# First block's feed-forward input as 24 units of seven half-size products, with two of the low halves made by GpSimd

## The reference, cut to what matters

```python
h = rmsnorm(x, norm_ffn[l])
x = x + conv_ffn(h, ffn_w_in[l], ffn_conv_w[l], ffn_conv_b[l], ffn_w_out[l])
```

## Time and profile before

| | |
|---|---|
| times of three runs | 2921.67, 2915.93 and 2917.06 us, median 2917.06 us |
| span of the profiled execution | 2915.5 us |
| its own time | given only among the three runs, not beside the span; the span is 1.6 us under their median |
| granted TensorE clock | 1.000 over the span (2.4 GHz level) |
| PE, PEld busy | 99%, 86% |
| DVE, ACT, POOL busy | 73%, 44%, 12% |

### The profile page before, as it was taken

How to read it: one execution, slowest core, us unless ns; L and a number is a source line. 1 busy time by engine, 2 the same in 40 slices (tenths; PEclk the granted TensorE clock), 3 DMA queues, 4 the chain that set the end, 5 groups by cost and what they waited for, 6 DMA issues and landing times.

```text
span 2915.5 us, 46310 instructions
## 1 busy us (share of the span) xinstructions
PE 2895.9 (99%) x16662; PEld 2505.6 (86%) x16662; DVE 2123.2 (73%) x3346; ACT 1275.7 (44%) x2027; POOL 356.7 (12%) x272
## 2 busy tenths in 40 slices
PE   9999999999999999999999999999999999999999
PEld 7888788778888888998887899988998887699987
DVE  8797674667766648888566887858888767688862
ACT  4653732342222225555233555625555236465541
POOL 0043340000000001110033011101110021011100
PEclk9999999999999999999999999999999999999999
DMA  4322123223323336773334477436774332257723
GB/s 142 98 94 94 58 95 122 73 80 125 98 94 96 99 94 170 184 185 101 108 109 130 122 182 184 118 109 173 187 184 110 103 109 80 80 156 179 187 78 108
DMA packets 129884, 356.97 MB, mean 122 GB/s; under 512 B 14608, under 2 KB 14864, under 8 KB 129360
## 3 DMA queue, kind: packets, MB, share of 16 engines
q1 hardware_dynamic: 103248, 303.14, 32.1%
q0 software_dynamic: 26496, 51.92, 10.4%
HBM read 352.90 MB, written 2.10 MB: 122 GB/s over the span
## 4 chain that ended last, share of the span: by engine, by line
PE 56%; DVE 3%; issue 1%; ACT 1%; DMA 1%; POOL 0%; DVEq 0%; SPq 0%; POOLq 0%; ACTq 0%
PE ps L1443 9%; PE ps L1445 9%; PE ps L1444 9%; PE ps L993 9%; PE ps L995 8%; PE ps L994 8%; PE ps L1667 0%; PE ps L1704 0%; PE ps L1158 0%; DMA cpad<-in_pairs 0%; PE ps L1147 0%; PE ps L1670 0%; DVE w_lo L2581 0%; DVE region_low L3177 0%; PE ps L1133 0%
## 5 line engine op out<-in xcount | busy, mean ns | idle before, releaser
L1778 ACT ACTIVATE w_hi<-raw 128x1024 fp32r<-128x1024 f32 x348 | 366.7, 1055 | 434.1 <-DMA raw<-in_wstream 434.0
L993 PE MATMUL ps<-h_hi,w_hi 128*128 128x512 f32 (+1 forms) x1267 | 497.3, 392 | 2.9 <-DVE w_lo L2581 1.7
L995 PE MATMUL ps<-h_hi,w_lo 128*128 128x512 f32 (+1 forms) x1267 | 490.1, 387 | 0.0
L994 PE MATMUL ps<-h_lo,w_hi 128*128 128x512 f32 (+1 forms) x1267 | 489.9, 387 | 0.0
L2581 DVE TENSOR_TENSOR w_lo<-raw,w_hi 128x1024 fp32r<-128x1024 f32 x268 | 324.6, 1220 | 110.1 <-ACT w_hi L1778 98.7
L1443 PE MATMUL ps<-h_hi,w_hi 128*128 128x256 f32 x1056 | 300.3, 284 | 0.6 <-DVE w_lo L3187 0.4
L1444 PE MATMUL ps<-h_lo,w_hi 128*128 128x256 f32 x1056 | 298.8, 283 | 0.0
L993 PEld LDWEIGHTS ps<-h_hi,w_hi 128*128 128x128 f32 x1267 | 238.0, 188 | 57.3 <-issue 6.1
L994 PEld LDWEIGHTS ps<-h_lo,w_hi 128*128 128x128 f32 x1267 | 238.1, 188 | 49.2 <-issue 2.2
L995 PEld LDWEIGHTS ps<-h_hi,w_lo 128*128 128x128 f32 x1267 | 237.9, 188 | 48.6
L907 POOL TENSOR_TENSOR w_lo<-raw,w_hi 128x1024 fp32r<-128x1024 f32 x78 | 196.0, 2517 | 495.0 <-ACT w_hi L1778 485.4
(11 more groups left out here) (684 smaller groups left out, 7354.2 us busy)
## 6 DMA issues: line engine op xcount, KB each, us to landing
raw<-in_wstream SPq DMA_DIRECT2D x349, 512.0 KB, 3.5
region<-in_pairs SPq DMA_DIRECT2D x121, 256.0 KB, 4.3
region<-in_pairs POOLq DMA_DIRECT2D x76, 256.0 KB, 5.7
last_pairs<-in_pairs SPq DMA_DIRECT2D x66, 256.0 KB, 3.9
raw<-in_pairs SPq DMA_DIRECT2D x22, 512.0 KB, 5.4
region<-in_pairs SPq DMA_DIRECT2D x22, 512.0 KB, 5.9
last_pairs<-in_pairs SPq DMA_DIRECT2D x22, 512.0 KB, 5.4
last_pairs<-in_pairs POOLq DMA_DIRECT2D x44, 256.0 KB, 5.4
```

The source lines that it names most:

```text
L993: nc.tensor.matmul(dst, hi_w, hi_x, start=first, stop=False)
L994: nc.tensor.matmul(dst, hi_w, lo_x, start=False, stop=False)
L995: return nc.tensor.matmul(dst, lo_w, hi_x, start=False, stop=last)
L1778: nc.scalar.activation(w_hi[:, n % HL], raw[:, r], ACT.Copy).then_inc(hi_ready, 1)
```

## The change

The input product of the first block becomes a fifth `HalfProducts`, called `inner`, of 24 units, with `convolved=True`. The stage `f1_in` and its 48 panels go; its weights come as unit pieces like the others'. What differs from the other four:

- DVE no longer makes the low halves of t3 and t4. GpSimd does (`pool_low_t3`, `pool_low_t4`, 128 x 512 each), in its queue between the issues of the accumulating transfers.
- DVE makes the three taps of unit u-1 inside unit u, from a scaled gate tile in `cpad`, spread over the order of `convolved_unit`. unit_mid moves to two units behind, and ACT's GELU comes behind high_c.
- ACT's copy of P5 waits for the gated tile of two units before.
- The eight panels of `wo` come in another order, and x is added from a reloaded copy as before.
- The up half is not multiplied by the root of the norm; each of the 8 tiles of `f1_out` is, by one more DVE operation.

```diff
-    ("wo", 8, 8, 8), ("f1_in", 48, 48, 24), ("f1_out", 24, 8, 8),
+    ("wo", 8, 8, 8), ("f1_out", 24, 8, 8),
...
+            def low_by_pool(self, kind):
+                return self.convolved and kind in ("t3", "t4")
...
+            def pool_low_t3(f, u, i=None):
+                pool.wait_ge(t3_high, f.nth(u + 1, i))
+                nc.gpsimd.tensor_tensor(f.unit_low("t3", u % 2), f.unit_raw("t3", u % 2), f.unit_high("t3").bitcast(F32), ALU.subtract)\
+                    .then_inc(t3_low, 1)
...
+                def unit(u, i=None):
+                    if u + 1 < f.units:
+                        sum_t3(f, u + 1, i)
+                    pool_low_t3(f, u, i)
+                    pool_low_t4(f, u, i)
+                    if u + 2 < f.units:
+                        sum_t1(f, u + 2, i)
...
+                def tap(u, k, i=None):
+
+                    p = u % 2
+                    src, w = cpad[:, p, 2 + k:2 + k + S], vcol("ffn_conv_w", F1 * k + u, i, 2)
+                    if k == 0:
+                        if u:
+                            dve.wait_ge(c21_taken, f.nth(u + 1, i))
+                        else:
+                            dve.wait_ge(gate_scaled, f.index + 1)
+                        v.tensor_scalar(tmp[:, p], src, w, vcol("ffn_conv_b", u, i, 2), ALU.mult, ALU.add).then_inc(conv_tap, 1)
+                        return
+                    dve.wait_ge(conv_tap, at(2 * u + k, i, 4))
+                    v.scalar_tensor_tensor(out=tmp[:, p], in0=src, scalar=w, in1=tmp[:, p], op0=ALU.mult, op1=ALU.add)\
+                        .then_inc(conv_tap if k == 1 else conv_done, 1)
...
+                def convolved_unit(u, i=None):
+                    second_right(u - 1, i)
+                    if u == 2 and i is None:
+                        first_gate()
+                        low_b21(2)
+                        first_right(1)
+                        tap(0, 0)
+                        low_t2(2)
+                        tap(0, 1)
+                        low_c(2)
+                        tap(0, 2)
+                    else:
+                        first_right(u - 1, i)
+                        low_t2(u, i)
+                        unit_mid(u - 2, i)
+                        low_c(u, i)
+                    second_left(u - 1, i)
+                    sum_t2(u + 1, i)
+                    tap(u - 1, 0, i)
+                    first_left(u, i)
+                    tap(u - 1, 1, i)
+                    left_scaled(u, i)
+                    if u == 2 and i is None:
+                        unit_mid(0)
+                    between_right(u, i)
+                    sum_t4(u + 1, i)
+                    tap(u - 1, 2, i)
+                    low_b11(u + 1, i)
+                    low_t1(u + 1, i)
+                    low_b21(u + 1, i)
...
+                    if u >= 2 and f.convolved:
+                        act.wait_ge(mid_made, f.nth(u - 1, i))
                     nc.scalar.activation(stage[:, p, right], f.unit_bank(p, 1), ACT.Copy).then_inc(p5_copied, 1)
...
+                    if u > 1 and f.convolved:
+                        unit_gate(u - 1, i)
...
+                src = stage[:, (st.s + c) % 2]
+                done(v.tensor_tensor(src, src, rstd[:], ALU.mult))
+                v.tensor_tensor(xt, xt, src, ALU.add).then_inc(posted, 1)
...
+            def beside_f1_out(c, part):
+                last_of_inner(c, part)
+                beside_first(c, part)
```

More of the change, by code:

```diff
@@ L429, in build, with __init__ @@
         class HalfProducts:
-            def __init__(self, nth, entry, gain, rms, before, after, x_rooms, raw, low, raw_b, room, rounds, gated, gated_hi, gated_lo):
-                self.base, self.index, self.entry, self.before, self.after = UNITS * nth, nth, entry, before, after
+            def __init__(self, nth, entry, gain, rms, before, after, x_rooms, raw, low, raw_b, room, rounds, gated, gated_hi, gated_lo,
+                         convolved=False):
+                self.base, self.index, self.entry, self.before, self.after = BASES[nth], nth, entry, before, after
+                self.units, self.convolved = len(gated), convolved
                 self.gain, self.rms, self.x_rooms, self.raw, self.low, self.raw_b = gain, rms, x_rooms, raw, low, raw_b
@@ L862, in _ @@
             other_units(first)
-            sp.wait_ge(p2_done, first.nth(UNITS - 1))
+            sp.wait_ge(p2_done, first.nth(first.units - 1))
             load(st.n + 20)
@@ new lines, in sums_and_lows @@
+            def sums_and_lows(f):
+                def unit(u, i=None):
[5 more added lines that the diff above has]
+                        sum_t1(f, u + 2, i)
+                unit_sums(f, 0)
+                sum_t1(f, 1)
+                unit(0)
+                unit(1)
+                with pool.Fori(0, f.rounds) as i:
+                    for u in (2, 3):
+                        unit(u, i)
+                for u in range(2 + 2 * f.rounds, f.units):
+                    unit(u)
@@ L1515, in seven_products @@
                         unit(u, i)
-                for u in range(2 + 2 * f.rounds, UNITS):
+                for u in range(2 + 2 * f.rounds, f.units):
                     unit(u)
-                pe.wait_ge(c21_taken, f.nth(UNITS - 1))
-                gemm(out, f.gated_hi, f.gated_lo, (mid_split, lambda k: f.base + k + 1), F2, between=((KB - 2, lambda: fourth(UNITS - 1)),))
+                pe.wait_ge(c21_taken, f.nth(f.units - 1))
+                gemm(out, f.gated_hi, f.gated_lo, (mid_split, lambda k: f.base + k + 1), f.units,
+                     between=((KB - 2, lambda: fourth(f.units - 1)),))
+            seven_products(inner, "f1_out")
             seven_products(first, "s0a_out")
@@ L2101, in _ @@
             gemm("br2", to_stage("br2"))
[L2102 to L2119, removed]
-                        if first and i is None and o == pr == 0:
-                            first()
-                        ready(2 * o + pr, i)
-                        nc.scalar.activation(tmp[:, s % 2], tmp[:, s % 2], func).then_inc(act_done, 1)
-                repeat(act, name, 4, body, peel=first is not None)
-            gates("f1_in", ACT.Gelu_apprx_tanh,
-                  lambda c, i: act.wait_ge(conv_done, at(CV["f1_in"] + c + 1, i, 2)), lambda: root_and_split("f1_in"))
             def seven_products(f):
@@ L2359, in all_units @@
                             unit(u, i)
-                    for u in range(2 + 2 * f.rounds, UNITS - 1):
+                    for u in range(2 + 2 * f.rounds, f.units - 1):
                         unit(u)
@@ L3476, in all_units @@
                     done(v.reciprocal(f.rms[:, right], f.rms[:, right]))
-                    unit(2)
-                    unit(3)
+                    one_unit = convolved_unit if f.convolved else unit
+                    one_unit(2)
+                    one_unit(3)
                     with dve.Fori(0, f.rounds - 1) as i:
                         for u in (4, 5):
-                            unit(u, i)
-                    for u in range(2 + 2 * f.rounds, UNITS - 1):
-                        unit(u)
+                            one_unit(u, i)
+                    for u in range(2 + 2 * f.rounds, f.units - 1):
+                        one_unit(u)
                         if f is first and u == 17:
@@ L3501, in last_unit @@
                     low_t2(u)
+                    if f.convolved:
+                        unit_mid(u - 2)
                     low_c(u)
@@ L3509, in last_unit @@
                     between_right(u)
-                    unit_mid(u - 1)
+                    if f.convolved:
+                        tap(u - 1, 2)
+                    else:
+                        unit_mid(u - 1)
                     split(f.after.n)
```

248 lines of the change are left out of this document (137 added, 111 removed).

## The result

| | before | after |
|---|---|---|
| median of four runs each | 2916.5 us | 2949.64 us (2949.14 to 2951.02) |
| ratio | | 1.0112, 95% interval 1.0100 to 1.0124 |
| profiled execution: time, span | span 2915.5 us | 2949.4 us, 2947.7 us |

The change makes the kernel slower by 33 us. The direction and the mechanism were forecast, and the size was not: 16 us were forecast (2933), and 2949.6 is outside the range of 2905 to 2943.

A forecast was written before the change was run, and what follows sets the result against it. TensorE was taken to bound the kernel (PE busy 99%). Fewer matmuls -17.0, steady units +23.0, entry +5.0, exit +4.3 and root multiply +0.7 gave +16.0 us: about 2933, range 2905 to 2943.

The forecast's parts named there:

- steady unit, 20 of them: Units 3 to 22: 11.2 us each, 1.15 above TensorE's pace through blocked DVE operations, 23.0 in all.
- entry up to P1(3): First units: unit 2 stalls on ACT's copies and t3's low half, low_b11(3) comes later; 5.0 us, bounds 2.5 to 6.5.
- last unit: Unit 23: P7 1.2 us late behind taps and a blocked left_scaled, f1_out's first low panel 0.45 late.
- f1_out, over the 131.79 of before: Output product: takes in the last unit's P4 (1.4 us), a 1.10 split stall and later DVE work.
- f1_out's root multiply: Multiplying f1_out's tiles by the root: hidden for seven tiles, on the path for the eighth, 0.7 us.
- the exit's 4.3: Last unit and f1_out: late P7, late splits and interrupted gated low halves, 4.3 us together, bounds 2 and 6.
- 1.86 for both, between 1.6 and 2.0: Steady unit: us that GpSimd's two low halves add to DVE's stretch from P4's end to low_b11.
- 0.76 before P1: Steady unit: us of slack between the undisturbed end of DVE's stretch (9.29) and P1(u+1) at 10.05.
- The rule of two SBUF inputs: DVE operations on two SBUF tiles stand until GpSimd's SBUF-reading operation ends; those on PSUM and one tile run on.
- halves cost nothing: Rival: GpSimd's halves fall on PSUM operations or DVE's waits; units of 10.05, 2906 us; chance 0.15.
- half collision: Rival: one of the two halves lands in free time; unit 10.3, 2913 us; chance 0.13.
- mutual blocking rival: GpSimd also waits for DVE, making low_t3 or unit_mid late; unit about 11.8, 2945 us; chance 0.12.

The follow-up runs named there:

- kernel 7: Experiments 6 with t4's low half moved to GpSimd, late (after next unit's low_b21) and behind the t1 sum; 2911.11 us.
- kernel 4: Changed kernel with t4's low half made by VectorE behind low_b21, only t3's half left on GpSimd; 2932.67 us.
- kernel 3: Changed kernel with GpSimd's t4 half waiting for next unit's low_b21 and the t1 sum issued ahead of that half; 2932.95 us.
- kernel 8: Changed kernel with next unit's low_b11 ahead of the third tap, both halves still on GpSimd; 2962.20 us.
- kernel 9: As kernel 8, with first_left also moved ahead of sum_t2; 2949.37 us.
- Experiment 5: Changed kernel with both low halves (t3, t4) made by VectorE, GpSimd only issuing transfers; 2914.13 us.
- Experiments 6: As Experiment 5, with next unit's low_b11 ahead of the third tap; 2909.02 us.
- experiments 1: Changed kernel with each GpSimd half cut to a 16-column subtraction plus clearing of the other 496 columns; 2908.56 us.

## Why the prediction was wrong in its size

The difference in the spans is 32.2 us, and the sum of the forecast was 16.0. By its own steps:

| step | forecast | measured |
|---|---|---|
| steady unit, 20 of them | 11.2 | 11.91: 14.2 us more |
| entry up to P1(3), third's 30.97 plus | 5.0 | 7.1 |
| last unit, third's 10.73 plus | 1.65 | 1.8 |
| f1_out, over the 131.79 of before | 5.15 | 4.32 |
| `wo`, start of P1(0) | 0 | 0.96 |
| f1_out's root multiply (`first`'s length) | 0.7 | 0.70 |

(The entry of third is 1701.10 - 4.62 less 1655.45 and less one unit of 10.06, its last unit what 18 more units leave up to 1878.23. The 4.62 are explained below. The 5.15 are the P4 of 1.4, the 1.10 and 2.65 of the exit's 4.3. The rows are 16.6 above the forecast's; the part behind `first` is 0.2 shorter than before, and 0.2 are roundings of the forecast.)

**The step that failed** is the length of the steady unit, "1.86 for both, between 1.6 and 2.0" and the "0.76 before P1". It accounts for 14.2 of the 16.2 us. The wait, VectorE standing beside GpSimd's halves, was the right one; two terms of it were mis-sized, about evenly. The halves cost 2.2 in the mean where 1.86 was put, and the slack was 0.38 where 0.76 was put.

**The price of the halves.** It was read off one row, L2640's 0.98, as if every half cost that. The rows of the experiments say what that 0.98 was made of. Each loss is the length of a DVE row less 0.68 (0.69 for the first); the lead is how far ahead GpSimd started; 0.12 is the 0.68 less the 0.56 by which DVE's row ended behind GpSimd's:

| where | GpSimd holds | lead | held - lead - 0.12 | loss |
|---|---|---|---|---|
| before, 2289.45 | 1.35 | 0.24 | 0.99 | 0.98 |
| kernel 7, 850.79 | 1.29 | 0.49 | 0.68 | 0.66 |
| kernel 4, 853.74 | 1.61 | 0.18 | 1.31 | 1.31 |
| kernel 3, 852.98 | 1.60 | 0.05 | 1.43 | 1.42 |
| after, 858.83 | 1.26 + 1.60 | 0.64 | 2.10 | 2.10 |
| kernel 8, 849.72 | 1.26 + 1.61 | 0.04 | 2.71 | 2.69 |

So here DVE stands until the GpSimd row ends, the pair counts as one hold from the start of the first to the end of the second, and what is left of the hold when DVE comes is what is lost. In the changed kernel and kernels 3, 4, 8 and 9 every blocked sum_t2 of the stage ended 0.54 to 0.57 behind the end of the last GpSimd row that it stood for. A half of 1.35 with a lead of 0.24 was a good row for the rule and a poor one for the price: in the stage a half that follows a transfer's issue takes 1.6, and the pair 2.86. The forecast also let the first half run partly under first_left. The t3 sum was issued at 3.76 into the unit, not 5.0, so the halves began at 4.3, beside sum_t2, and nothing of them fell on an operation that reads PSUM. With sum_t2 at 2.77 to 3.13 the loss was 2.1 to 2.45, not 1.86.

**The slack.** P4's result came 4.62 after the start of P1 (854.51 to 859.13), not 4.31, which counted matmul slots alone. With another 0.07 for the end of low_b11 and its signal the stretch had 0.38 before P1, not 0.76. 4.62, the ten operations' 5.05 and the block of 2.10 make 11.77, which is that unit (854.51 to 866.28). Experiment 5 tests the same number without GpSimd: 9.7 and a low half of 0.60 are 10.3, and 10.3 was measured. Experiments 6 and 7, with 0.66 less ahead of P1, run at 10.08.

**The entry** was 2.1 more. With both halves on VectorE (5) it is 34.7 by the same measure, third's 30.97 and 3.8; the GpSimd halves make the other 3.3. The stalls of unit 2 are the ones forecast: P6's wait for ACT's copy (PEld idle 2.13) and P7's for the half of t3 (1.99) make 4.1 where 4.8 was put, and 0.76 before P1(3) stands against 0.9. What the forecast lacked is 1.27 at 754.34, before P7 of unit 1, which waits for between_right (L3403), and small waits in the first 11 us, 2.2 together against third's 1.0. Which part of the 3.8 stands on which operation was not tried. The 0.96 of `wo` shows in all eleven profiles of the new form (the stage starts at 732.3 to 733.2, not 731.86), and its cause was not looked for.

**What was right.** TensorE's pace of 10.05 to 10.08 once nothing blocks, and no loss from loads. The rule of two SBUF inputs, as far as it goes: first_left (0.40 to 0.43) is never longer, sum_t2 is in every steady unit. The rival "halves cost nothing" gave 2906 for a unit of 10.05, and experiments 1 and 6, with such a unit, took 2908.6 and 2909.0. Its premise on GpSimd was wrong; its sum for the rest was 3 us off. The half collision's unit of 10.3 occurs in 5 for another reason. The mutual blocking rival had the measured time nearly (2945 for a unit of 11.8) by a mechanism that didn't occur: in every steady unit read DVE was the one that stood, and neither the gate nor the copy of P5 was late in a steady unit.

The Trainium skill ("SBUF — State Buffer", Who interferes with whom) says that the one that issues first has the port for the whole instruction and that issue order, not shape, decides who blocks. The table agrees: GpSimd started first in all six rows, and a half of the same shape cost 0.66 in one place and 1.42 in another. By the starts in the rows it does not hold everywhere, as the last section shows. The Trainium skill also says to time GpSimd by the spacing of its starts and not by its rows ("Perfetto Trace Analysis", GPSIMD Engine Instruction). For the pace that holds (1.26 apart, rows of 1.6). For the block it does not: the last row's end is what the losses follow.

## What to carry to other kernels

Price a GpSimd operation beside VectorE not by the loss of one row but by when it will end and what VectorE has behind it: a half that held VectorE for 0.66 in its slack left the unit at 10.08, and one at the front of the bound stretch cost 1.3 to 1.4 and made it 11.1 to 11.2. Reckon with the case that two GpSimd operations that are both ready hold as one; they did in this stage, though not in the rows of before below. Before work is moved off VectorE, add up whether it fits: here both halves fitted on VectorE once the one TensorE waits for was put first, and that made 2909 of 2917.8, where the change with the halves on GpSimd had cost 33 us. A result in PSUM comes later than its last matmul's slot, and 0.3 us of that counts in a stretch with less than 1 us to spare.

## What the runs showed of the hardware that was not expected

- DVE, ready and waiting, was not served between two GpSimd operations 1.26 us apart (859.47 to 862.25 after). That is not so everywhere. In the kernel before, in the run of four 1024-element low halves of the earlier trace rows, the DVE operation of the earlier trace rows at 1486.12 ended at 1488.54, behind the second of them and well ahead of the end of the third:

```profile
1485.58 2.41 POOL L907 TENSOR_TENSOR w_lo<-raw,w_hi 128x1024 fp32r<-128x1024 f32 x1
1487.95 2.86 POOL L907 TENSOR_TENSOR w_lo<-raw,w_hi 128x1024 fp32r<-128x1024 f32 x1
```
```profile
1488.58 2.52 DVE L2676 TENSOR_SCALAR tmp<-cpad,vec 128x512 f32<-128x512 f32 x1
```

  DVE was served between the two there, and the third, which overlapped it, took 2.86 in place of 2.41. The rows of these overlap by 0.04, those of the stage's pair by 0.36; whether that, the length or something else decides was not tried.
- VectorE operations with a single SBUF tile as input stood still too, where the tensor_scalar of tap 0 came up beside GpSimd's read. One unit of kernel 8, DVE and GpSimd:

```profile
838.37 3.12 DVE L3444 TENSOR_SCALAR tmp<-cpad,vec 128x512 f32<-128x512 f32 x1
```
```profile
838.36 1.62 POOL L988 TENSOR_TENSOR region_low<-region,w_hi 128x512 fp32r<-128x512 f32 x1
839.61 1.59 POOL L993 TENSOR_TENSOR region_low<-region,w_hi 128x512 fp32r<-128x512 f32 x1
```

  3.12 in place of 0.54: with tap 0 in that place the pair costs nearly what it costs with sum_t2 there. Kernel 1's tap 0 took 0.97 beside a memset that reads nothing (852.98 and 853.09, above). The forecast held only operations on two SBUF tiles to be exposed. The rows of before could have told it: the tensor_scalar at 1488.58 (above) took 2.52 where one takes 0.55.
- The start in the row is not always what decides. In 13 units of kernels 3, 4 and 8 sum_t2 started 0.01 to 0.33 ahead of the half's row and stood until 0.56 after its end all the same. In a unit of kernel 4 the second tap started 0.41 ahead of GpSimd's row and still stood until 0.56 after that row's end (2.59 in place of 0.74):

```profile
776.26 2.59 DVE L3446 SCALAR_TENSOR_TENSOR tmp<-cpad,vec,tmp 128x512 f32<-128x512 f32 x1
```
```profile
776.67 1.62 POOL L988 TENSOR_TENSOR region_low<-region,w_hi 128x512 fp32r<-128x512 f32 x1
```

  With a lead of -0.41 the formula of the table gives 1.91, and the loss is 1.85. In two cases sum_t2 lost nothing: 0.59 ahead of the pair in kernel 8 (at 837.77), and 0.30 ahead of the 16-column subtraction in kernel 1. What separates these from the others is open.
- The granted clock fell below 1.00 in windows of the stage in kernels 8 and 9: kernel 8 as shown, kernel 9 to 0.91 over 850 to 870 us, where its one unit of 13.77 lies. It costs about 1.6 us in each unit concerned of kernel 8 (13.6 in place of 12.0) and 2 in that of kernel 9. PEld's pause in most steady units was 1.7 to 2.1 in kernel 8, 1.5 to 1.8 in kernel 9, and 1.4 to 1.7 in the changed kernel, which stayed at 1.00. That the pauses brought the clock down was not tested, and their length alone does not settle it: in unit 2 both the changed kernel and kernel 8 pause for 2.13 and 1.99, and then the clock is 1.00 in the one and 0.50, the 1.2 GHz level, in the other (770 to 772 us).
